# Norm sums of a one-core decoder step with the squares as the stationary operand

## What is computed

```
def rms_norm(x, g):
    xf = x.astype(jnp.float32)
    y = xf * lax.rsqrt(jnp.mean(xf * xf, axis=-1, keepdims=True) + EPS)
    return (y * g.astype(jnp.float32)).astype(x.dtype)
...
    xp = xp + g_mp[:, None, :] * rms_norm(op, norm_mix_post[i])
...
    hp = modulate(xp, norm_ffn_pre[i], sh_fp, sc_fp)
```

## Time and profile before

| | |
|---|---|
| median of three runs | 3035.55 us |
| lowest, highest | 3034.37, 3038.49 us |
| span of the profiled execution | 3035.5 us, 42942 instructions |
| own time of the profiled execution | none is given beside its span |
| PE busy | 2788.4 us (92%), 15550 products |
| VectorE busy | 1785.9 us (59%) |
| ACT busy | 1028.9 us (34%) |
| two FFN stages | 872.7 and 879 us of the span |

### The profile page before, as it was taken

How to read it: one execution, slowest core, us unless ns; L and a number is a source line. 1 busy time by engine, 2 the same in 40 slices (tenths; PEclk the granted TensorE clock), 3 DMA queues, 4 the chain that set the end, 5 groups by cost and what they waited for, 6 DMA issues and landing times. The chain is left out here.

```text
span 3035.5 us, 42942 instructions
## 1 busy us (share of the span) xinstructions
PE 2788.4 (92%) x15550; PEld 2386.6 (79%) x15550; DVE 1785.9 (59%) x3148; ACT 1028.9 (34%) x1692; POOL 99.8 (3%) x71
## 2 busy tenths in 40 slices
PE   6979699999978897999999999985799999999996
PEld 2568577777755775999999999933499999999993
DVE  3961455555632216666666666656666666666665
ACT  5832233333321224333223323233432333333232
POOL 0000000000000002000000000014200000000001
PEclk8989899999979998999999999997899999999998
DMA  7910100000044201111111111000111111111101
GB/s 296 419 59 24 47 11 11 20 11 0 0 163 147 108 8 42 43 57 47 41 41 41 41 41 41 33 21 8 42 42 42 41 41 41 53 51 42 41 28 64
DMA packets 42729, 178.46 MB, mean 59 GB/s; under 512 B 6146, under 2 KB 9730, under 8 KB 38690
## 3 DMA queue, kind: packets, MB, share of 16 engines
q1 hardware_dynamic: 41938, 176.81, 16.0%
q10 hardware_dynamic: 720, 0.71, 0.1%
HBM read 170.43 MB, written 7.07 MB: 58 GB/s over the span
## 5 line engine op out<-in xcount | busy, mean ns | idle before, releaser
L1875 DVE TENSOR_TENSOR ffn_y<-psum,ffn_y 128x384 f32<-128x384 f32 (+1 forms) x1056 | 555.0, 534 | 496.1 <-PE psum L1935 495.3
L1933 PE MATMUL psum<-ffn_h_hi,ffn_w_hi 128*128 128x384 f32 (+1 forms) x2112 | 694.1, 329 | 15.7 <-DVE ffn_h_lo L431 15.7
L1934 PE MATMUL psum<-ffn_h_lo,ffn_w_hi 128*128 128x384 f32 (+1 forms) x2112 | 696.2, 330 | 0.0
L1935 PE MATMUL psum<-ffn_h_hi,ffn_w_lo 128*128 128x384 f32 (+1 forms) x2112 | 693.3, 328 | 0.0
L1933 PEld LDWEIGHTS psum<-ffn_h_hi,ffn_w_hi 128*128 128x128 f32 x2112 | 399.7, 189 | 16.6 <-DVE ffn_h_lo L431 16.3
L1934 PEld LDWEIGHTS psum<-ffn_h_lo,ffn_w_hi 128*128 128x128 f32 x2112 | 399.9, 189 | 0.0
L1935 PEld LDWEIGHTS psum<-ffn_h_hi,ffn_w_lo 128*128 128x128 f32 x2112 | 399.7, 189 | 0.0
L1933 PE MATMUL psum<-ffn_g_hi,ffn_w_hi 128*128 128x384 f32 (+1 forms) x1056 | 357.7, 339 | 19.8 <-DVE ffn_g_lo L1896 15.1
L1934 PE MATMUL psum<-ffn_g_lo,ffn_w_hi 128*128 128x384 f32 (+1 forms) x1056 | 347.1, 329 | 0.0
L1935 PE MATMUL psum<-ffn_g_hi,ffn_w_lo 128*128 128x384 f32 (+1 forms) x1056 | 346.9, 328 | 0.0
L1785 ACT ACTIVATE ffn_u<-psum 128x384 f32<-128x384 f32 (+1 forms) x264 | 119.7, 453 | 549.0 <-PE psum L1935 443.4
(11 more groups left out here) (233 smaller groups left out, 3691.4 us busy)
## 6 DMA issues: line engine op xcount, KB each, us to landing
ffn_raw<-in_ffn_w SPq DMA_DIRECT2D x132, 512.0 KB, 5.1
ada_w<-in_ada_w SPq DMA_DIRECT2D x24, 2048.0 KB, 10.9
cache<-in_cache SPq DMA_DIRECT2D x64, 320.0 KB, 4.8
x<-in_x SPq DMA_DIRECT2D x2, 4352.0 KB, 17.6
pair_raw<-in_pair_w SPq DMA_DIRECT2D x8, 768.0 KB, 4.4
wo_raw<-in_wo SPq DMA_DIRECT2D x8, 512.0 KB, 4.0
proj_raw<-in_proj_w SPq DMA_DIRECT2D x7, 512.0 KB, 3.7
out_x_out<-x SPq DMA_DIRECT2D x2, 1536.0 KB, 6.0
```

The costliest lines, as they stand in the source:

```text
L1875: dve.tensor_tensor(dst, down_bank[i % 2][:, 0:n_], dst, ALU.add).then_inc(acc_done, 1)
L1933: pe.matmul(bank[:, a], w_hi[s][:, w], act_hi, start=first, stop=False)
L1934: pe.matmul(bank[:, a], w_hi[s][:, w], act_lo, start=False, stop=False)
L1935: return pe.matmul(bank[:, a], w_lo[s][:, w], act_hi, start=False, stop=last)
```

## The change

The sums are made with the squares as the stationary operand, 128 tokens at a time, and the column of ones moving. Three products per channel tile accumulate into three columns of the same bank, one sum per partition. Only the first product of a job clears the bank. The root is taken on this 128x3 column block (in the third chunk, whose last column has 64 rows, in two instructions) into a new tile std, and the reciprocal reads that. The turning products, their semaphore and the row are gone. ACT's root waits for the reciprocal of the job before in place of its turning, and PE's sum always waits for the root of the job before.

```diff
--- before.py
+++ after.py
@@ -57,7 +57,6 @@
         self.squared = s("squared")
         self.summed = s("summed")
         self.std = s("std")
-        self.turned = s("turned")
         self.rstd = s("rstd")
         self.spread_done = s("spread")
         self.groups = []
@@ -88,44 +87,39 @@
 
     def act_root(self, k, act, j):
         src, c, _ = self.jobs[j]
-        n = CHUNKS[c][1]
         act.wait_ge(self.summed, self.groups_to[j])
         if j:
-            act.wait_ge(self.turned, j)
-        act.activation(k.row[:, 0:n], k.stat_bank[0:1, 0:n], ACT.Sqrt, scale=1.0 / (src.shape[1] * P),
-                       bias=k.eps[0:1, :]).then_inc(self.std, 1)
+            act.wait_ge(self.rstd, j)
+        tiles = col_tiles(c)
+        rows = tiles[-1][1]
+        scale = 1.0 / (src.shape[1] * P)
+        if rows == P:
+            act.activation(k.std[:], k.stat_bank[:, 0:3], ACT.Sqrt, scale=scale, bias=k.eps[:]).then_inc(self.std, 1)
+        else:
+            act.activation(k.std[:, 0:2], k.stat_bank[:, 0:2], ACT.Sqrt, scale=scale, bias=k.eps[:])
+            act.activation(k.std[0:rows, 2:3], k.stat_bank[0:rows, 2:3], ACT.Sqrt, scale=scale,
+                           bias=k.eps[0:rows, :]).then_inc(self.std, 1)
 
     def pe(self, k, pe, j):
         self.pe_sum(k, pe, j)
-        self.pe_turn(k, pe, j)
 
     def pe_sum(self, k, pe, j):
-        n = CHUNKS[self.jobs[j][1]][1]
         first = self.groups_to[j - 1] if j else 0
         tiles = sum(w for _, w, _, _ in self.groups[j])
-        if j and k.col_bank is k.stat_bank:
-            pe.wait_ge(self.rstd, j)
-        elif j:
+        if j:
             pe.wait_ge(self.std, j)
         for i, (g, w, slot, _) in enumerate(self.groups[j]):
             pe.wait_ge(self.squared, first + i + 1)
             for t in range(w):
-                last = pe.matmul(k.stat_bank[0:1, 0:n], k.ones[:, 0:1], k.sq[:, 3 * slot + t, 0:n],
-                                 start=g + t == 0, stop=g + t == tiles - 1)
+                for col, (o, rows) in enumerate(col_tiles(self.jobs[j][1])):
+                    last = pe.matmul(k.stat_bank[0:rows, col:col + 1], k.sq[:, 3 * slot + t, o:o + rows],
+                                     k.ones[:, 0:1], start=g + t == 0 and col == 0, stop=g + t == tiles - 1,
+                                     skip_group_check=True)
             last.then_inc(self.summed, 1)
 
-    def pe_turn(self, k, pe, j):
-        pe.wait_ge(self.std, j + 1)
-        if j:
-            pe.wait_ge(self.rstd, j)
-        for i, (o, w) in enumerate(col_tiles(self.jobs[j][1])):
-            last = pe.matmul(k.col_bank[0:w, MAXC + i:MAXC + i + 1], k.row[0:1, o:o + w], k.ones[0:1, 0:1],
-                             start=True, stop=True)
-        last.then_inc(self.turned, 1)
-
     def dve(self, k, dve, j):
-        dve.wait_ge(self.turned, j + 1)
-        dve.reciprocal(self.jobs[j][2], k.col_bank[:, MAXC:MAXC + 3]).then_inc(self.rstd, 1)
+        dve.wait_ge(self.std, j + 1)
+        dve.reciprocal(self.jobs[j][2], k.std[:]).then_inc(self.rstd, 1)
 
     def pe_spread(self, k, pe, j, bank):
         pe.wait_ge(self.rstd, j + 1)
@@ -158,12 +152,12 @@
         self.rstd = self.sbuf(ctx, "rstd", [P, 3, NC, 3])
         self.psum = ctx.enter_context(nc.psum_tensor("psum", [P, 8, 512], F32))
         self.banks = [self.psum[:, i, :] for i in range(8)]
-        self.stat_bank, self.col_bank = self.banks[6:8]
+        self.std = self.sbuf(ctx, "std", [P, 3])
+        self.stat_bank = self.banks[6]
 
     def norm_work(self, flat):
 
         self.sq = flat[:, 0:NORM_WORK].rearrange("p (k t) -> p k t", k=5)
-        self.row = flat[0:1, NORM_WORK:NORM_WORK + MAXC]
 
     def sbuf(self, ctx, name, shape, dt=F32):
         return ctx.enter_context(self.nc.sbuf_tensor(name, shape, dt))
@@ -304,8 +298,6 @@
                         last.then_inc(used, 1)
                 if not (first and s == 0):
                     turn(m - 1, (s - 1) % ADA_SLOTS, first)
-                if first and s >= X_JOBS:
-                    x_norm.pe_turn(k, pe, s - X_JOBS)
             pe.wait_ge(parts, 2)
             pe.wait_ge(constants, 3)
             run(step, pe, lambda: x_norm.pe(k, pe, NC - 1))
@@ -542,7 +534,6 @@
         for c in range(NC):
             if not (summed and c == 0):
                 self.norm.pe_sum(k, pe, c)
-            self.norm.pe_turn(k, pe, c)
             self.norm.pe_spread(k, pe, c, banks[c])
         if self.stats:
             for c in range(NC - 1):
@@ -614,7 +605,6 @@
         ROPE_UNIT = LT
         banks = [k.banks[0:3], k.banks[3:6]]
         kv_spread, q_spread = k.banks[7], banks[1]
-        k.col_bank = k.stat_bank
         Q_LAST = UNITS - 1
         block = own.enter_context(nc.Block())
 
@@ -745,16 +735,16 @@
 
             side = {
                 (first, 0): lambda: kv_norm.pe_sum(k, pe, 0),
-                (first, 1): lambda: (kv_norm.pe_turn(k, pe, 0), kv_norm.pe_sum(k, pe, 1)),
-                (first, 2): lambda: (kv_norm.pe_turn(k, pe, 1), kv_norm.pe_sum(k, pe, 2), kv_spread_chunk(0)),
-                (second, 0): lambda: (kv_norm.pe_turn(k, pe, 2), kv_spread_chunk(1)),
+                (first, 1): lambda: kv_norm.pe_sum(k, pe, 1),
+                (first, 2): lambda: (kv_norm.pe_sum(k, pe, 2), kv_spread_chunk(0)),
+                (second, 0): lambda: kv_spread_chunk(1),
                 (second, 1): lambda: kv_spread_chunk(2),
 
                 (Q_LAST, 0): lambda: (pe.wait_ge(kv_norm.rstd, NC), q_norm.pe_sum(k, pe, 0)),
-                (Q_LAST, 1): lambda: (q_norm.pe_turn(k, pe, 0), q_norm.pe_sum(k, pe, 1)),
-                (Q_LAST, 2): lambda: (q_norm.pe_turn(k, pe, 1), q_norm.pe_sum(k, pe, 2),
+                (Q_LAST, 1): lambda: q_norm.pe_sum(k, pe, 1),
+                (Q_LAST, 2): lambda: (q_norm.pe_sum(k, pe, 2),
                                       pe.wait_ge(evac_a, NC * (UNITS - 2)),
-                                      q_norm.pe_spread(k, pe, 0, q_spread[0]), q_norm.pe_turn(k, pe, 2),
+                                      q_norm.pe_spread(k, pe, 0, q_spread[0]),
                                       q_norm.pe_spread(k, pe, 1, q_spread[1]), q_norm.pe_spread(k, pe, 2, q_spread[2])),
             }
             for j in range(UNITS):
@@ -783,7 +773,6 @@
 
 def mla_prompt_stage(k, m):
 
-    k.col_bank = k.banks[7]
     nc, io = k.nc, k.io
     STEPS = 2 * QB
     with ExitStack() as own:
@@ -1511,7 +1500,7 @@
         scaled_s = pooled[:, :, SEQ:NT]
         a = k.ada[:, 1, SCALE_MIX:SCALE_MIX + KT, :]
         b = k.ada[:, 1, SHIFT_MIX:SHIFT_MIX + KT, :]
-        k.stat_bank, k.col_bank = k.banks[6:8]
+        k.stat_bank = k.banks[6]
         late = last_x_norm(k, "pool_in")
         exit_ = Exit(k, "pool_out", 1, GATE_MIX, y)
         w_in, const_in, zeroed = k.sem("pool_w_in"), k.sem("pool_const_in"), k.sem("pool_zeroed")
@@ -1726,7 +1715,7 @@
         state_out = k.sem(n + "state_out")
         half_bank = [k.banks[0:3], k.banks[3:6]]
         down_bank = k.banks[6:8]
-        k.stat_bank, k.col_bank = half_bank[G][0:2]
+        k.stat_bank = half_bank[G][0]
         block = own.enter_context(nc.Block())
 
         @block.sync
```

## The result

The changed kernel takes 3112.85 us (median of 4 runs, 3109.98 to 3115.08), the kernel before beside it 3034.96 us (4 runs, 3032.14 to 3038.49): a ratio of 1.0255, 95% interval 1.0241 to 1.027, or +78 us. The forecast was slower, 3085 us, with a range up to 3110; the result lies just above it. The execution profiled took 3111.77 us, its span is 3110.0.

What follows compares the result with a forecast made beforehand. TensorE (PE), busy 92% of the span, was taken to set the pace in the exits. Terms 12.1 + 10.5 + 11.4 + 5.0 + 8.7 - 1 + 1.2 + 1.2 = +49 on 3035.5 gave 3085 us, range 3050 to 3110.

Steps and rivals of the forecast that it cites:

- The level: New sums and the spreads between them: expected at 1.2 GHz, a sum costing 10.1 us against 5.3 at the high level.
- time full of weight loads did not raise it: Earlier trace, L1296: PE busy 3.00 of 3.00 us with 64 moving columns, clock stayed 0.50; hence 1.2 GHz expected in sums.
- stretch of turning products alone: Attention exit of the earlier trace, 1167.5 to 1171.2: the clock fell after it, read as following streaming of the moving operand.
- The price of a record: New sums: each record costs its weight load, 0.11 us at the full clock, 0.21 at 1.2 GHz.
- The tail: End of each norm job: root 0.2, reciprocal 0.15, no turning products; 0.6 instead of 1.75 us.
- 16 of half width, as 40: Sums of 320 column chunks: 32 full and 16 half-width records priced as 40, 4.4 us high or 8.4 low.
- rival A: Whole kernel: clock stays at 2.4 GHz, sums cost as before, tails shrink, VectorE binds the exits; 3007 us, 11%.
- job four (no spread, the next sum waits for the root alone) 10.5: Exit after pooling: the fourth job takes 10.5 us, as the fifth sum waits only for its root.
- I take 4, so 36 records at 0.11 and 12 at 0.21: 6.5 us: First sum of the exit after pooling: clock falls 4 us after the last streaming work, so the sum takes 6.5 us.
- The adaLN stage: First stage: slower sums and following products at the low clock, less three roots at -1.0; +8.7 us in all.
- +1.8 per group of products: AdaLN stage: products after a sum start at the low level, between +0 and +3.7 us, taken as +1.8.
- rival C: Low level spreads: q products and first products of each FFN stay at 0.50 some spells longer; 3100 to 3115 us, 6%.

Runs made afterwards that it cites:

- 128 columns: The changed kernel with 128 columns of ones moving instead of one, all weight loads kept: 3038.35 us, ratio 1.0017 to the kernel before.
- wide loads: 128 columns of ones moving, plus the third chunk's last load taking tokens 192 to 319 at full width: 3018.34 us, ratio 0.9949 to the kernel before.

## Why the forecast was right in sign and short in size

**The level: right, and the whole of the sign.** The step "time full of weight loads did not raise it", drawn from one line with 64 moving columns, held for one column too, and so did what L143 with 128 moving columns spoke for the earlier trace rows: the exits with 128 columns ran high. One of its rows showed less than was read from it: in the "stretch of turning products alone" (1167.5 to 1171.2) PE was busy for 0.80 of 3.70 us, so the fall behind it may as well be that of an idle engine. The Trainium skill, TensorE: Matmul & The Clock Gate, Part 1, has the clock follow how busy the PE has been. Here 9.70 us of 9.70 busy left it at 0.50, so in this kernel it did not follow PE's busy time as the profile counts it.

**The price of a record: right.** 0.213 against the 0.21 taken, at the high level 5.7 us a job with 128 columns against 5.3. The tail is right as well (in the changed kernel's pooling exit the first sum ends at 2175.51 and PE takes up the spread 0.63 later, 0.6 taken), with the root at 0.263 instead of 0.2. The second job of the exit measured 12.24 us for 12.0.

**Half-width loads priced as half: wrong.** The step "16 of half width, as 40", 8.4 us per 320 column job, measured 9.83. The narrow records of the spread behind it, taken as 1.1 us in all, made it 1.77 (2200.36 to 2202.13). So the third job of the exit, from sum to sum, took 12.31 us for 10.1. Four such sums and three such spreads lie in the exits: 5.7 + 2.0, near 8 us. It is also what hid the gain at the high level: 8.07 where 4.4 was written. The wide loads gave back 20 of the 31 us between the 3007 of rival A and the 3038 of the 128 columns. The rest is not taken apart; part of it is that rival A had VectorE bind the exit after pooling at 32 to 33 us, where with wide loads it takes 35.3 (2104.47 to 2139.78) and PE still sets its pace.

**The hand-over from the fourth to the fifth job: missed.** The step "job four (no spread, the next sum waits for the root alone) 10.5" measured 11.89 (2202.13 to 2214.02). ACT squares the fifth job's tiles only after the fourth root:

```profile
2212.56 0.26 ACT L97 ACTIVATE std<-psum,eps 128x3 f32<-128x3 f32 x1 [5.16 <-PE psum L115]
2212.72 1.89 ACT L85 ACTIVATE pool_work<-x 128x1152 f32<-128x1152 f32 x2
```

so PE stands still until 2214.02. The wait was in the earlier trace rows already, 0.32 us ahead of the fifth sum, "<-ACT"; it was read as slack of ACT. So the cost left out is that of ACT's squares, and three exits have it, 1.4 each: 4 us.

**When the clock falls: too late.** "I take 4, so 36 records at 0.11 and 12 at 0.21: 6.5 us". In the pooling exit it fell 1.2 us into the sum, in the attention exit 2.1 us, and these sums took 9.25 and 8.30. Together 4.6 us. PE had been idle for 1.90 us right before the pooling sum, but before the attention sum products streamed up to its start, so the idle stretch alone does not explain it. Nor does the single column in the pooling exit: with 128 columns the clock fell there 1.3 us into the same sum. What the 128 columns changed is that it came back. In the two FFN exits, where products stream until the sum, 6.07 and 6.17 us were measured for the 6.5.

**The adaLN stage: the right mechanism at half its size.** Forecast +8.7, measured +15.5. The sums took 10.40, 9.58 and 9.01 us; forecast were 10.3, 8.3 (7.01 and 1.3 more) and 6.2: the second and third I had costed as if they ran high for most of their length. That is 4.2 of the 6.8 us missing here. ACT squares only after PE has freed a slot, so the whole length of each sum stands in ACT's chain, as its idle times above show (3.94, 5.24, 7.97, 5.20). The +1.8 per group of products between them was chosen in the middle of 0 to 3.7; after the first sum the clock was low until 51.2 us, nearly to the last of the products (45.46 to 51.95, against 3.7 us before).

**The account.** Between the two profiled spans +74.5 was measured for +49, so 25.5 us are missing (the medians, 3.4 us further apart, are of other executions). The four exits lack 18.6: 8 for the narrow records, 4 for the hand-over, 4 for the clock (4.6, less what the FFN exits gained), and 2 to 3 not taken apart. The adaLN stage lacks 6.8, the projection stage 2.4, the pooling entry 2.4, the FFN entries 1.3. Against them stand the 6 us by which the unchanged stretches were shorter; why they were, no run shows, and executions of one kernel differ by as much (3032.14 to 3038.49).

The measured time lies in rival C's 3100 to 3115, but not for rival C's reason. Its first products of each FFN did not get slower: from the last reciprocal of the entry to the first sum of the exit the two FFNs took 816.8 and 817.2 us before and 814.4 and 816.0 after. Of its places only the projection stage was longer than forecast, by the 2.4 above.

## What to carry to other kernels

Before a small operand is swapped into the moving place, cost the clock as well as the loads: in all four exits of this kernel the clock fell among products with one moving column and stayed at 1.2 GHz to the exit's end, and each record of the sums took twice its time. If the data must stand still, try the moving column repeated to 128. It cost little at the same level (a q sum of 24 records took 2.81 us with one column and 2.91 with 128, both at 2.4 GHz), and it was the difference between +78 us and +5. And keep the loads of one width, even at the price of columns summed twice; only with both did the shorter tail come out, as -15 us.

## What the runs showed of the hardware

- The granted clock with loads back to back followed the moving columns: 1 and 32 the same (3112.85 and 3112.77 us), 128 high, and 64 (3099.56 us) high at first and then low. How long it stayed high with 64 differed from exit to exit: 2.4 us in the pooling exit (until 2154.2), 22.7 us and three sums in the attention exit. What decides that, no run here shows.
- A load of 64 columns among loads of 128 costs more than one of 128 at 2.4 GHz, and the more the more columns move: 8.07 against 5.61 us for 48 records with 128 moving columns, 6.82 against 5.67 with 64, and with one, in a q sum of 24 records, 3.01 against 2.81. At 1.2 GHz with one column it saves a little: 9.83 against 10.24. The old kernel's 320 column sum of 6.16 us is another matter: one spell at the low level lies in it, and the same sum takes 4.64 us without.

```profile
2133.60:2139.70 6.10, 6.10 (x17) 1.52 (x16) 5.38 (x11) 1.00 (x1) 4.45 (x4) 0.72 0.00 0
```

- Even with 128 columns a spell at the low level can come in. The first sum of the pooling exit, 7.22 us in one kernel and 5.78 in the other with the same instructions and the same 1.90 us of idle PE before it, has it in the one:

```profile
2116.20:2118.00 1.80, 1.80 (x14) 1.80 (x15) 0.00 (x0) 0.59 (x1) 0.00 (x0) 0.87 0.00 0
2118.00:2120.00 2.00, 2.00 (x11) 2.00 (x11) 0.00 (x0) 0.79 (x1) 0.00 (x0) 0.50 0.00 0
2120.00:2122.00 2.00, 2.00 (x16) 2.00 (x15) 0.00 (x0) 0.37 (x1) 0.00 (x0) 0.76 0.00 0
```

  The clock fell and rose again while the same 128 column products went on, which the sums with one column never did in this exit: there the low level held for 61.4 us from 2167.5 on.
